# Seven block products in place of eight in two chunk pairs of the last feed-forward stage

## The reference

```
x  = x + merged @ w_out
h2 = rmsnorm(x, norm_mlp_g)
up = square(relu(h2 @ w_up))       # 1024 x 4096
x  = x + up @ w_down               # 4096 x 1024
```

## Time and profile before

| | |
|---|---|
| median of 3 runs | 996.53 us (996.36 to 996.55) |
| span of the profiled execution | 994.1 us |
| TensorE busy | 99% |
| VectorE, ScalarE, GpSimd busy | 69%, 56%, 12% |

### The profile page before, as it was taken

The page is one execution under the profiler, slowest core; times in us unless marked ns, Lnnn a source line. Parts: engine busy times, 40 slices in busy tenths (PEclk is TensorE's granted clock), DMA queues, the critical chain, the costliest instruction groups (busy, mean ns, idle before and its releaser), DMA issues.

```text
span 994.1 us, 12539 instructions
## 1 busy us (share of the span) xinstructions
PE 987.6 (99%) x4608; PEld 810.6 (82%) x4608; DVE 682.7 (69%) x998; ACT 553.6 (56%) x761; POOL 118.6 (12%) x109
## 2 busy tenths in 40 slices
PE   8999999999999999999999999999999999999998
PEld 7788888888777788888888888888888888888887
DVE  6666566668987667656565678776689767656663
ACT  7444343577665546444444586868885555443542
POOL 0000000022300000000000041169904000000000
PEclk9999999999999999999999999999999999999999
DMA  7987776586444546766666487658555546777761
GB/s 263 284 266 255 234 250 211 193 305 196 140 152 143 169 130 214 227 198 214 211 204 226 156 229 237 176 163 212 151 191 196 202 156 204 228 223 227 226 198 43
DMA packets 165465, 201.44 MB, mean 203 GB/s; under 512 B 55969, under 2 KB 111658, under 8 KB 165290
## 3 DMA queue, kind: packets, MB, share of 16 engines
q1 hardware_dynamic: 164826, 200.69, 64.3%
q10 hardware_dynamic: 592, 0.14, 0.1%
HBM read 182.45 MB, written 5.77 MB: 189 GB/s over the span
## 4 chain that ended last, share of the span: by engine, by line
PE 96%; DVE 2%; ACT 1%; POOL 1%; issue 0%; ACTq 0%; POOLq 0%; DVEq 0%
PE bank L1969 23%; PE bank L1971 23%; PE bank L1970 23%; PE bank L2087 7%; PE bank L2086 7%; PE bank L2085 7%; PE bank L1984 1%; PE bank L2136 1%; PE bank L2251 1%; DVE lo L1348 0%; PE bank L2151 0%; PE bank L2138 0%; PE bank L2374 0%; PE bank L2375 0%; PE bank L2347 0%
## 5 line engine op out<-in xcount | busy, mean ns | idle before, releaser
L1969 PE MATMUL bank<-hi,xh 128*128 128x512 f32 (+1 forms) x944 | 374.8, 397 | 0.9 <-DVE lo L1574 0.8
L1971 PE MATMUL bank<-hi,xl 128*128 128x512 f32 (+1 forms) x944 | 367.2, 389 | 0.0
L1970 PE MATMUL bank<-lo,xh 128*128 128x512 f32 (+1 forms) x944 | 366.5, 388 | 0.0
L1331 DVE TENSOR_TENSOR lo<-raw,hi 128x2048 fp32r<-128x2048 f32 (+1 forms) x111 | 253.9, 2289 | 146.2 <-ACT hi L824 146.2
L824 ACT ACTIVATE hi<-raw 128x2048 fp32r<-128x2048 f32 (+1 forms) x114 | 216.5, 1901 | 133.7 <-PE bank L2087 97.0
L1969 PEld LDWEIGHTS bank<-hi,xh 128*128 128x128 f32 x944 | 177.3, 188 | 39.7 <-issue 2.5
L1971 PEld LDWEIGHTS bank<-hi,xl 128*128 128x128 f32 x944 | 177.2, 188 | 37.2
L1970 PEld LDWEIGHTS bank<-lo,xh 128*128 128x128 f32 x944 | 177.5, 188 | 34.4
L1348 DVE TENSOR_TENSOR lo<-raw,hi 128x1024 fp32r<-128x1024 f32 (+1 forms) x108 | 131.9, 1230 | 43.1 <-ACT hi L833 42.4
L2085 PE MATMUL bank<-hi,hh 128*128 128x512 f32 (+1 forms) x306 | 119.3, 390 | 0.0
L2087 PE MATMUL bank<-hi,hl 128*128 128x512 f32 (+1 forms) x306 | 118.7, 388 | 0.0
(11 more groups left out here) (271 smaller groups left out, 961.6 us busy)
## 6 DMA issues: line engine op xcount, KB each, us to landing
raw<-in_w_in SPq DMA_DIRECT2D x48, 1024.0 KB
raw<-in_ffn_w_gu SPq DMA_DIRECT2D x82, 512.0 KB
raw<-in_ffn_w_down SPq DMA_DIRECT2D x22, 1024.0 KB
raw<-in_w_up SPq DMA_DIRECT2D x16, 1024.0 KB
raw<-in_w_down SPq DMA_DIRECT2D x16, 1024.0 KB
raw<-in_w_out SPq DMA_DIRECT2D x8, 1024.0 KB
distance_table<-ftab SPq DMA_DIRECT2D x8, 576.0 KB
raw<-in_w_proj_attn SPq DMA_DIRECT2D x4, 1024.0 KB
```

What stands on the lines that cost most here:

```text
L1331: nc.vector.tensor_tensor(lo[s][:, :, 0:width], raw[s][:, :, 0:width], hi[s][:, :, 0:width].bitcast(F32), ALU.subtract).then_inc(lo_done, 1)
L1969: nc.tensor.matmul(o, sh, wh, start=first and j == 0, stop=False)
L1970: nc.tensor.matmul(o, sh, wl, start=False, stop=False)
L1971: ins = nc.tensor.matmul(o, sl, wh, start=False, stop=last and j == 3)
```

## The change

Four pairs of chunks make up the stage. In the pairs that begin at chunks 2 and 6 the up projection is a 2x2 by 2x2 block product: token tiles by K halves, and K halves by the two chunks. It is done by Winograd's form of Strassen's scheme with seven products p1 to p7 of 12 matmuls each in place of eight. Four of the products (p4 to p7) use sums of weight blocks, and four (p3, p5, p6, p7) use sums of blocks of the normalized input.

The parts of the edit are these.

- SP loads the four weight blocks of such a pair into operand tiles of their own (`last_operand`), which take memory that earlier stages used. For the first pair these loads stand among the loads of `U_P2` and wait for `k_rl` 2. Loads, flips and waits of the last stage are written out in one list.
- VectorE makes four sums of weight blocks per pair (`weight_sum`, 128x2048). The first two of the first pair stand ahead of `add_out(0, 0)` in the handover; the rest stand in the last stage. It makes the sums of the input once (`x_sums`, `sum_lo`), ahead of the splits of the stage, and per pair three adds of products (`add_product`).
- ScalarE now does relu, square and planes of all chunks (`plain_planes`, `square`), copies three products out of their bank per pair (`keep`), and writes the high parts of the input sums.
- Every product has a hi/lo unit of its own in the ring, so a pair has 11 units in place of 8. Seven of them are used for one token tile only.
- TensorE no longer transposes the last chunk, whose hidden values go by DMA transposes like the others'.
- The hidden values have twice the buffers (`last_hh`, `last_hl`), the loops of ScalarE and VectorE in this stage are written out, and some semaphores of earlier stages are shared with other constants.

```diff
+PAIRS = (2, 6)
+def last_order():
+    order = [("u", i, u) for i in range(2) for u in range(2)]
+    i = 2
+    while i < NF2:
+        d = [("d", i - 2 + c, b) for c in range(2) for b in range(2)]
+        if i in PAIRS:
+            p = {k: (k, i, 0) for k in OPERAND}
+            order += [p["p1"], p["p2"], d[0], p["p6"], d[1], p["p7"], p["p5"], p["p4"], d[2], p["p3"], d[3]]
+        else:
+            order += [("u", i, 0), ("u", i, 1), d[0], d[1], ("u", i + 1, 0), ("u", i + 1, 1), d[2], d[3]]
+        i += 2
+    return order + [("d", i, b) for i in (NF2 - 2, NF2 - 1) for b in range(2)]
...
 @block.sync
+            def last_operand(j, b):
+                half, chunk = b % 2, PAIRS[j] + b // 2
+                if j == 0:
+                    sp_eng.wait_ge(k_rl, 2)
+                else:
+                    sp_eng.wait_ge(lo_done, unit_of(("p1", "p4", "p7", "p3")[b], PAIRS[j - 1]) + 1)
+                    sp_eng.wait_ge(last.t_made, 4 * j - (3, 0, 1, 1)[b])
+                src = col_view(a["w_up_2"])[:, 4 * half:4 * half + 4, chunk * W:chunk * W + W]
+                sp_eng.dma_start(operand[b][:, :, :], src).then_inc(last.b_in[b], 16)
...
             for c in range(4):
                 for half in range(2):
                     columns(a["w_proj_attn_2" if c < 2 else "w_proj_rnn_2"], U_P2 + 2 * c + half, c % 2 * W, half)
+                    if (c, half) in ((2, 1), (3, 1)):
+                        last_operand(0, 2 * (c - 2))
             for c in range(2):
                 for half in range(2):
                     columns(a["w_out_2"], U_P2 + 8 + 2 * c + half, c * W, half)
+                    if (c, half) == (0, 1):
+                        last_operand(0, 3)
...
 @block.scalar
+            def plain_planes(i, t):
+                act.wait_ge(used, unit_of("u", i, 1) + 1) if t == 1 else act.wait_ge(last.g0, PLAIN.index(i) + 1)
+                if i == 0:
+                    act.wait_ge(n_rstd, 2 * last.norm + t + 1)
+                step(nc.scalar.activation(hid[:, t, :], (G, X)[i % 2][t][:, :], ACT.Relu, scale=rstd_x[:, t:t + 1]),
+                     last.acted)
+                step(nc.scalar.activation(hid[:, t, :], hid[:, t, :], ACT.Square))
+                planes_from(i, t, hid[:, t, :])
+            def pair_chunks(j):
+                i = PAIRS[j]
+                last_split_hi(unit_of("d", i - 2, 0))
+                keep(j, 0)
+                last_split_hi(unit_of("p6", i))
+                last_split_hi(unit_of("d", i - 2, 1))
+                square(j, 0)
+                last_split_hi(unit_of("p7", i))
+                last_hi(i - 1)
+                keep(j, 1)
+                last_split_hi(unit_of("p5", i))
+                last_split_hi(unit_of("p4", i))
+                keep(j, 2)
+                last_split_hi(unit_of("d", i - 1, 0))
+                last_split_hi(unit_of("p3", i))
+                square(j, 1)
+                last_split_hi(unit_of("d", i - 1, 1))
+                square(j, 2)
+                last_split_hi(unit_of("d", i - 1, 1) + 1)
+                last_split_hi(unit_of("d", i - 1, 1) + 2)
+                square(j, 3)
+                last_hi(i)
+            def last_ffn():
+                plain_planes(0, 0)
+                last_split_hi(U_L + 3)
+                plain_planes(0, 1)
+                last_split_hi(U_L + 4)
+                for m in (1, 3, 2, 4):
+                    sum_hi(m)
+                last_split_hi(U_L + 5)
+                last_hi(0)
+                plain_planes(1, 0)
+                plain_planes(1, 1)
+                for i in range(2, NF2, 2):
+                    if i in PAIRS:
+                        pair_chunks(PAIRS.index(i))
+                    else:
+                        plain_chunks(i)
...
 @block.vector
+            def pair_chunks(j):
+                i = PAIRS[j]
+                last_split_lo(unit_of("d", i - 2, 0))
+                add_product(j, 0)
+                last_split_lo(unit_of("p6", i))
+                last_split_lo(unit_of("d", i - 2, 1))
+                last_merge(i - 1)
+                if j == 0:
+                    weight_sum(j, 3)
+                last_split_lo(unit_of("p7", i))
+                weight_sum(j, 4)
+                last_lo(i - 1)
+                last_split_lo(unit_of("p5", i))
+                last_split_lo(unit_of("p4", i))
+                last_split_lo(unit_of("d", i - 1, 0))
+                add_product(j, 1)
+                last_split_lo(unit_of("p3", i))
+                last_split_lo(unit_of("d", i - 1, 1))
+                last_merge(i)
+                last_split_lo(unit_of("d", i - 1, 1) + 1)
+                add_product(j, 2)
+                last_split_lo(unit_of("d", i - 1, 1) + 2)
+                last_lo(i)
+            def last_ffn():
+                x_sums()
+                last_split_lo(U_L + 3)
+                last_split_lo(U_L + 4)
+                for m in (1, 3, 2, 4):
+                    sum_lo(m)
+                last_merge(0)
+                last_split_lo(U_L + 5)
+                last_lo(0)
...
             split_lo(U_P2 + 12)
+            weight_sum(0, 1)
+            weight_sum(0, 2)
             add_out(0, 0, p_y0, U_P2 + 8)
             add_out(0, 1, p_y0, U_P2 + 8)
             last_columns(4, p_y0, U_P2 + 8, U_L)
-            ffn(ffns[2])
+            last_ffn()
```

## The result

The changed kernel takes 1013.6 us (median of 4 runs, 1011.92 to 1015.28); beside it the kernel before took 996.54 us (996.36 to 996.71). The ratio is 1.0172, 95% interval 1.0157 to 1.0186. The profiled execution has a span of 1010.4 us, 16.3 us more than before.

What follows compares the result with a forecast made beforehand. TensorE, 99% busy at full clock, was taken as the bound. Five added waits, 18.8 us, less 6.2 of removed work, gave +12.6 on a 996.5 us median: 1009.1 us, range 1002 to 1016.

Steps and rivals of the forecast that it cites:

- B: Handover: two weight sums ahead of add_out delay the residual adds and TensorE's norm transposes; 4.4 us, bounds 4.2 to 4.6.
- A: Near 780 us: SP's wait for k_rl 2 delays the loads of U_P2+6 and +7, so TensorE waits; 5.3 us.
- C: First down unit: ScalarE's planes and input sums make its split late; TensorE waits 4.9 us, bounds 3.9 and 5.7.
- D: First pair's fifth product, p5: VectorE's queue with the third weight sum makes its lo late; 2.2 us, bounds 0 and 3.
- E: Chunk 6's hidden values, behind the second pair: planes wait for a flip, d(6,0) starts late; 2.0 us.
- Removed work: TensorE loses 24 matmuls (5.44 us) and the last chunk's eight transposes (0.79 us); together 6.2 us, all on the path.
- The clock: TensorE's clock may fall to 1.2 GHz after the long waits; none taken for the forecast, bound +5.4 us.
- rival 1: TensorE's clock falls after the waits, 2.72 us more each at A, B and C, C's swallowed by D: 1014.5 us; 28%.
- Rivals 2, 3, 4: Half the waits covered, 1002.9 us, 14%; all covered, 990.3 us, 7%; 0.25 us cost per product, 1012.6 us, 6%.
- rival 3: Stage entry: queued work fills ScalarE's and VectorE's gaps, lookahead covers the rest; 990.3 us with no waits, 7%.

Runs made afterwards that it cites:

- fix_all: fix_abce with the first pair's third weight sum moved out of the pair, behind the first two residual adds: 990.64 us, 0.9943 of the kernel before.
- fix_a: Changed kernel with loads of operands 0, 2 and 3 moved later in SP's list, behind U_P2+8, +9 and +10: 1006.84 us, ratio 1.0106.
- fix_b: Changed kernel with the first two weight sums moved from ahead of add_out(0,0) to behind chunk 0's hidden low part: 1007.93 us, ratio 1.0116.
- fill: Changed kernel with 49 useless 128x512 matmuls on TensorE inside the three long waits, no wait removed: 1010.8 us, ratio 1.0142.
- fix_c: Changed kernel with chunk 1's second-tile planes behind the first down unit's hi, and chunk 0's merge ahead of the four sum_lo: 1009.71 us, ratio 1.0138.
- fix_abce: Changed kernel with edits of fix_a, fix_c and fix_e, first two weight sums in VectorE gaps ahead of the residual adds: 995.68 us, ratio 0.9991.
- fix_e: Changed kernel with the next chunk's high parts ahead of square 3 and low parts ahead of the second split, both pairs: 1010.77 us, ratio 1.0145.

## Why the prediction was right or wrong

The direction, the range and the places hold; the number falls 4.5 us short. In the profiled execution the miss is 3.7 us (a span of 1010.4 against 1006.7): 2.3 at B by the clock, 1.2 at A by a load that landed late, 0.3 ahead of A, and near nothing at C, D and E together. The other 0.8 us is that the median of the runs lies 3.2 us above that span and not 2.4; its cause is not shown.

- **Removed work, 6.2 us.** Right; fix_all gives 6.3.
- **A, 5.3 predicted, 6.5 measured.** The mechanism is shown by fix_a. One part was short: the second of two loads landed near 780.1 and not 779.0, and everything behind it, to the end of the second gated product (789.5 and not 788.4), is late by as much. The half clock behind the wait cost nothing, since VectorE was later.
- **B, 4.4 predicted, 6.7 measured.** The wait itself is right (4.2 to 4.3). The rest is clock: 0.8 in the transposes, 1.6 in the 24 matmuls behind. fix_b removes it.
- **C, 4.9 predicted.** 4.6 by the wait, and 2.2 by the clock. The unknown term, planes on ScalarE, was 1.06 us against 1.05 taken.
- **D, 2.2 predicted, nothing in the changed kernel.** It is there wherever C's wait or its clock cost is gone: 1.7 us in fill, 3.4 with the wait at p7 in fix_c and fix_abce. The prediction's 2.2 is for the case of fill, with C's wait in front. The prediction said that C's clock cost would be swallowed by D, and so it was: C and D are 6.8 us together where 7.1 were forecast.
- **E, 2.0 predicted, 2.1 measured.** The place in the queue is shown by fix_e. The closeness is partly luck: the flips of that stretch landed after 2.7 to 2.8 us and not 3.5, for which the prediction had 1.3, and ScalarE came 0.8 us later than reckoned to the square ahead of the planes, so its own queue and not the flip set them.
- **The clock.** This is the step that was mis-sized most. "I take none for the forecast" put the cost at zero; it was rival 1, which gave 1014.5 with 28%, and 1013.6 came. That it came so near is in part luck: the rival's +5.4 was 2.7 us each after A and B, and the traces have nothing at A and 2.4 at B; after C there are 2.2, which D swallows as the rival said. Fill takes out 2.8 us by the medians. The trace of before had no wait that could show it. The Trainium skill said it ("TensorE: Matmul & The Clock Gate", "What's actually happening": an idle TensorE falls to 1.2 GHz), and the traces here agree: 0.50 behind waits of 4.2 to 4.4 us, and 1.00 where these waits were filled.
- **Rivals 2, 3, 4.** Half the waits covered, all covered, or a cost per product: none. That both engines work in program order, so that nothing moves into their gaps by itself, was the right objection to rival 3; filled by hand (fix_all), they give the time of rival 3, 990.3 against 990.64.

## What to carry to other kernels

When an engine is busy 99%, a cut in its work is worth its length only if everything that is added elsewhere finds a gap; shares of busy time can't tell, but the in-order queues can be walked through with durations from the trace, and here that gave each wait to within about a microsecond. Look first at what a new instruction or a new wait is placed in front of: two adds of 2.3 us ahead of a handover cost 6.7 us, and one semaphore wait in the load queue cost 6.5 us through loads that it had nothing to do with. A wait of 4 us on TensorE can cost more than its length, but only where nothing else sets the pace behind it: the half clock cost 2.4 us at B, nothing at A, where VectorE was later anyway, and at C 2.2 us, of which 1.7 would have been lost at D anyway (fill). And removing one bottleneck shows the next one behind it.

## What the runs showed of the hardware

- TensorE's clock fell to half behind waits of 4.2 to 4.4 us at A, B and C, and it was back within 8 us. Behind shorter waits it fell in some executions only: behind E's 2.1 us in the profile of fix_b and not in that of the changed kernel, and behind 0.8 and 2.6 us in fix_abce's and not in fix_c's, which has the same two. The spread of the runs goes with it: the mean granted clock was 0.990 to 0.995 in the changed kernel's runs, which spread over 3.4 us, and 1.000 in all five of fix_all, which spread over 0.4; in fix_abce it was 1.000 in the three shortest of ten and 0.998 in the others.
- Useless matmuls of 128x512 inside the waits kept the clock at full there and made the kernel 2.8 us faster by the medians.
- ScalarE copies 1024 16-bit elements in 1.06 us, no faster than 1024 of f32, while VectorE does them in 0.69 us.
- Loads of 1 MB queued one behind the other landed about 2.5 us apart; the second, issued 0.4 us behind the first, was there 7.5 us after its issue, against 4.5 us for a lone one. The landings are read from the starts of ScalarE's hi, 780.11 and 782.64.
